# Marks for expert gates: comparisons one step ahead of the dots, Pool's low halves in quarters, sixteen dots moved

## The reference, cut to what matters

```
def peer_ffn(x, wq, subkeys, u, v):
    q = (xt @ wq).reshape(t_len, PEER_HEADS, 2, PEER_QDIM // 2)
    sub = einsum('thpd,hpkd->thpk', q, subkeys)          # 8 heads, 2 halves, 128 keys
    s_top, i_top = top_k(sub, 16)
    cand = s_top[:, :, 0, :, None] + s_top[:, :, 1, None, :]
    sc, ci = top_k(cand.reshape(t_len, 8, 256), 16)
    i1 = take_along_axis(i_top[:, :, 0], ci // 16); i2 = take_along_axis(i_top[:, :, 1], ci % 16)
    eid = i1 * 128 + i2                                  # 128 experts for each token
    gate = softmax(sc)
    h = gelu(einsum('cd,ced->ce', xc, u[eid]))
    return einsum('ce,ced->cd', gate * h, v[eid])
```

## Time and profile before

| what | us |
|---|---|
| median of three runs | 1715.17 |
| the profiled execution | 1707.7 |
| its span | 1705.9 |
| PE busy | 1651.9 (97%) |
| VectorE busy | 1251.1 (73%) |
| ScalarE busy | 691.9 (41%) |
| Pool busy | 831.9 (49%) |
| PE's mean granted clock | 0.988 of full speed |

### The profile page before, as it was taken

The page is one execution under the profiler, slowest core; times in us unless marked ns, Lnnn a source line. Parts: engine busy times, 40 slices in busy tenths (PEclk is TensorE's granted clock), DMA queues, the critical chain, the costliest instruction groups (busy, mean ns, idle before and its releaser), DMA issues.

```text
span 1705.9 us, 24150 instructions
## 1 busy us (share of the span) xinstructions
PE 1651.9 (97%) x9013; PEld 1449.1 (85%) x9013; DVE 1251.1 (73%) x2462; ACT 691.9 (41%) x1030; POOL 831.9 (49%) x492
## 2 busy tenths in 40 slices
PE   9999999999999998899989989999999999999997
PEld 7778777788899998899989988999888888888886
DVE  3586894421255795999999999535888888888886
ACT  4545545422324344343443434333433333333332
POOL 6332233344633676776876677785524223332312
PEclk9999999999999999999999999999999999999999
DMA  5121122242422566997899689997999999999952
GB/s 203 63 75 62 50 75 74 87 148 87 161 74 71 177 208 236 343 379 233 291 379 364 222 290 367 375 372 284 394 401 354 375 382 358 375 376 353 385 200 86
DMA packets 126499, 417.61 MB, mean 245 GB/s; under 512 B 12976, under 2 KB 32432, under 8 KB 124848
## 3 DMA queue, kind: packets, MB, share of 16 engines
q1 hardware_dynamic: 70320, 232.81, 38.2%
q0 software_dynamic: 36864, 134.23, 21.0%
q10 hardware_dynamic: 19200, 49.03, 7.5%
HBM read 364.91 MB, written 50.86 MB: 244 GB/s over the span
## 4 chain that ended last, share of the span: by engine, by line
PE 76%; DVE 12%; DMA 5%; POOL 3%; issue 2%; ACT 2%; ACTq 0%; SPq 0%; DVEq 0%; POOLq 0%
PE ps L1362 14%; PE ps L1364 13%; PE ps L1363 13%; PE ps L1622 10%; PE ps L1621 10%; PE ps L1624 10%; DMA u_got<-u_rows,eid 4%; DVE right L1256 3%; DVE u_got L1126 2%; POOL w_lo L503 1%; PE ps L1474 1%; PE ps L1426 1%; POOL w_lo L459 1%; DMA raw<-w_units 1%; PE ps L1733 1%
## 5 line engine op out<-in xcount | busy, mean ns | idle before, releaser
L1362 PE MATMUL ps<-tok_hi,w_hi 128*128 128x384 f32 (+1 forms) x1472 | 531.1, 361 | 1.5 <-issue 1.5
L1364 PE MATMUL ps<-tok_hi,w_lo 128*128 128x384 f32 (+1 forms) x1472 | 521.7, 354 | 0.0
L1363 PE MATMUL ps<-tok_lo,w_hi 128*128 128x384 f32 (+1 forms) x1472 | 521.6, 354 | 0.0
L560 ACT ACTIVATE w_hi<-raw 128x1024 fp32r<-128x1024 f32 x330 | 349.2, 1059 | 391.0 <-PE ps L1624 288.4
L503 POOL TENSOR_TENSOR w_lo<-raw,w_hi 128x1024 fp32r<-128x1024 f32 x128 | 322.7, 2523 | 113.7 <-ACT w_hi L560 112.4
L459 POOL TENSOR_TENSOR w_lo<-raw,w_hi 128x1024 fp32r<-128x1024 f32 x76 | 182.2, 2401 | 315.0 <-ACT w_hi L560 314.9
L1362 PEld LDWEIGHTS ps<-tok_hi,w_hi 128*128 128x128 f32 x1472 | 280.4, 190 | 32.0 <-issue 12.3
L520 POOL DMA_INDIRECT v_got<-v_rows,eid x128 | 153.9, 1203 | 300.1 <-DVE own L1138 281.7
L1621 PE MATMUL ps<-w_hi,gh_hi 128*128 128x512 f32 x760 | 295.7, 389 | 0.0
L1622 PE MATMUL ps<-w_lo,gh_hi 128*128 128x512 f32 x760 | 295.7, 389 | 0.0
L1364 PEld LDWEIGHTS ps<-tok_hi,w_lo 128*128 128x128 f32 x1472 | 279.8, 190 | 18.1
(11 more groups left out here) (247 smaller groups left out, 1806.2 us busy)
## 6 DMA issues: line engine op xcount, KB each, us to landing
raw<-u_units SPq DMA_DIRECT2D x128, 512.0 KB, 4.7
raw<-v_rows SPq DMA_DIRECT2D x128, 512.0 KB, 6.7
raw<-w_units SPq DMA_DIRECT2D x78, 512.0 KB, 3.4
gate_d<-stage ACTq DMA_DIRECT2D x12, 2048.0 KB, 10.6
gelu_d<-gelu_t ACTq DMA_DIRECT2D x120, 192.0 KB, 4.7
gelu_in<-gelu_d SPq DMA_DIRECT2D x30, 768.0 KB, 8.1
gate_in<-gate_d SPq DMA_DIRECT2D x28, 768.0 KB, 12.5
gate_in<-gate_d SPq DMA_DIRECT2D x2, 1536.0 KB, 17.0
```

The source lines that it names most:

```text
L560: act.activation(hi_of(n), raw[:, n % RAW, :], ACT.Copy).then_inc(hi_done, 1)
L1362: pe.matmul(out_, l_hi, r_hi, start=start, stop=False)
L1363: pe.matmul(out_, l_hi, r_lo, start=False, stop=False)
L1364: return pe.matmul(out_, l_lo, r_hi, start=False, stop=stop)
```

## The change

Three edits. Pool makes each low half of the expert units in four subtractions of 256 columns; only the last tells the others. VectorE's `mark` is cut in two: `mark(m)` makes the comparisons (`match`, `left`), `times_gates(m)` the two products; in a mark stage the comparisons of mark m + 1 stand right behind the products of mark m, ahead of the dots of that unit. A semaphore of its own tells TensorE that `left` is set. The dots of the mark stages go from 30 to 26 each, those of routing tiles 2 and 3 from six to four; what is left comes in the tail.

```
+LO_PARTS = 4
-ROUTE_DOTS, MARK_DOTS = (3, 6, 6), 30
+ROUTE_DOTS, MARK_DOTS = (3, 4, 4), 26
...
                 pool.wait_ge(hi_done, n + 1)
-                pool.tensor_tensor(w_lo[:, n % RAW, :], raw[:, n % RAW, :], w_hi[:, n % RAW, :].bitcast(F32),
-                                   ALU.subtract).then_inc(lo_pool, 1)
+                for a in range(LO_PARTS):
+                    cols = slice(a * DM // LO_PARTS, (a + 1) * DM // LO_PARTS)
+                    ins = pool.tensor_tensor(w_lo[:, n % RAW, cols], raw[:, n % RAW, cols],
+                                             w_hi[:, n % RAW, cols].bitcast(F32), ALU.subtract)
+                ins.then_inc(lo_pool, 1)
...
+            def spread(a, m):
+
+                first = MARKED * (m % (P // MARKED))
+                return marks[:, a, first:first + MARKED].rearrange("p (g t) -> p g t", t=2).unsqueeze(2)\
+                    .to_broadcast([P, MARKED // 2, P, 2])
+
             def mark(m):
 
                 if m == 0:
                     dve.wait_ge(numbers_set, 1)
                 if m >= 3:
                     dve.wait_ge(gate_full, 2 * (m - 2))
                 if m >= 2:
                     dve.wait_ge(right_set, m - 1)
-                dve.tensor_tensor(match[:, m % 2], each, second, ALU.is_equal).then_inc(match_set, 1)
-                dve.tensor_tensor(left[:, s], each, first, ALU.is_equal)
+                each = numbers[:].unsqueeze(1).to_broadcast([P, MARKED // 2, P, 2])
+                dve.tensor_tensor(match[:, m % 2], each, spread(1, m), ALU.is_equal).then_inc(match_set, 1)
+                dve.tensor_tensor(left[:, m % 3], each, spread(0, m), ALU.is_equal).then_inc(left_set, 1)
+
+            def times_gates(m):
+
                 dve.wait_ge(match_set, m + 1)
                 for i in range(PIECES):
-                    ins = dve.tensor_tensor(right[i][:, s], match[:, m % 2], gate[i], ALU.mult)
+                    ins = dve.tensor_tensor(right[i][:, m % 3], match[:, m % 2], spread(2 + i, m), ALU.mult)
                 ins.then_inc(right_set, 1)
...
                 spread_picks(b)
+                mark(P // MARKED * (b - 1))
                 for k in range(MARK_UNITS):
-                    mark(P // MARKED * (b - 1) + k)
+                    m = P // MARKED * (b - 1) + k
+                    times_gates(m)
+                    if k + 1 < MARK_UNITS:
+                        mark(m + 1)
                     dots_to(dots_by(routed_at(b) + ROUTE_UNITS + k))
...
             def gates_of(q):
 
                 s = q // 2 % 3
+                pe.wait_ge(left_set, q // 2 + 1)
                 pe.wait_ge(right_set, q // 2 + 1)
```

More of the change, by code:

```diff
@@ L307, in peer_block @@
         "route_step", "gexp_in", "gexp_done", "pick_set", "pickT_full", "pickT_set"))
-    match_set, right_set, gate_full, gate_read, marks_step, numbers_set = (sem(n) for n in (
-        "match_set", "right_set", "gate_full", "gate_read", "marks_step", "numbers_set"))
+    match_set, left_set, right_set, gate_full, gate_read, marks_step, numbers_set = (sem(n) for n in (
+        "match_set", "left_set", "right_set", "gate_full", "gate_read", "marks_step", "numbers_set"))
     stage_out = [sem(f"stage_out{i}") for i in range(2)]
@@ L1238, in spread_picks @@
                 dve.wait_ge(marks_step, 2 * b)
+            def spread(a, m):
+                first = MARKED * (m % (P // MARKED))
+                return marks[:, a, first:first + MARKED].rearrange("p (g t) -> p g t", t=2).unsqueeze(2)\
+                    .to_broadcast([P, MARKED // 2, P, 2])
             def mark(m):
-                s, tok = m % 3, slice(MARKED * (m % (P // MARKED)), MARKED * (m % (P // MARKED)) + MARKED)
                 if m == 0:
@@ L1246, in mark @@
                     dve.wait_ge(gate_full, 2 * (m - 2))
-                first, second, *gate = (marks[:, a, tok].rearrange("p (g t) -> p g t", t=2).unsqueeze(2)
-                                        .to_broadcast([P, MARKED // 2, P, 2]) for a in range(2 + PIECES))
-                each = numbers[:].unsqueeze(1).to_broadcast([P, MARKED // 2, P, 2])
                 if m >= 2:
                     dve.wait_ge(right_set, m - 1)
-                dve.tensor_tensor(match[:, m % 2], each, second, ALU.is_equal).then_inc(match_set, 1)
-                dve.tensor_tensor(left[:, s], each, first, ALU.is_equal)
+                each = numbers[:].unsqueeze(1).to_broadcast([P, MARKED // 2, P, 2])
+                dve.tensor_tensor(match[:, m % 2], each, spread(1, m), ALU.is_equal).then_inc(match_set, 1)
+                dve.tensor_tensor(left[:, m % 3], each, spread(0, m), ALU.is_equal).then_inc(left_set, 1)
+            def times_gates(m):
                 dve.wait_ge(match_set, m + 1)
                 for i in range(PIECES):
-                    ins = dve.tensor_tensor(right[i][:, s], match[:, m % 2], gate[i], ALU.mult)
+                    ins = dve.tensor_tensor(right[i][:, m % 3], match[:, m % 2], spread(2 + i, m), ALU.mult)
                 ins.then_inc(right_set, 1)
```

## The result

The changed kernel takes **1768.82 us** (median of four runs, 1763.97 to 1769.71) against 1712.01 for the kernel before in the same comparison: ratio **1.0321** (95% interval 1.027 to 1.0372). It is 3.2% slower; the forecast was 1696. The profiled span is 1767.6 us against 1705.9.

The account below looks back on a forecast made before the run. PE was held up in the mark stages by VectorE, stalled by Pool's subtraction, with DMA a second limit. Marks -30 and tail +11 gave -19: 1707.7 to 1689, plus 7.5 for the median, 1696 us; range 1672 to 1716.

Parts of the forecast that it names:

- part one: Pool's expert low half in four pieces: 2.95 us instead of 2.40, a waiting VectorE instruction losing at most 0.74 instead of 2.4.
- I take one piece, 0.74: VectorE's stall per mark from Pool's pieces, chosen as 0.74 us between bounds of 0 and 2.95.
- A waiting engine is served next: At the port VectorE and Pool share: Pool got in between two adjoining VectorE instructions, so whichever engine waits goes next.
- Part two, order: Mark stages: comparisons moved ahead of the dots bring `right` 1.28 us earlier; the new waits on `gate_full` and `left_set` cost nothing.
- Part three, dots in the marks: Mark stages with 26 dots instead of 30: VectorE 5.5 us a unit, 87 us a stage; 30 us won.
- The wait for picks at the head of stage 3: Third mark stage's head unit takes 11.87 us instead of 5.15, PE waiting for routing's picks; these 6.7 us would go.
- DMA as second limit: Mark stages: DMA share 0.91 to 0.95, busy time with fewer dots 90.4, 85.6, 91.8 us; gain between 23 and 36 us.
- full pace: Rival: DMA carries it and mark units reach PE's 5.15 us; -52 + 6 gives 1669 us; chance 0.15.
- Tail: Last expert units: 16 added dots load Pool (4.95 to 5.50 us a unit) and DMA; 11 us lost, bounds 4 and 20.
- Turn by turn: Rival: most mark operations wait for a piece each, VectorE needs 6.9 us a unit; 1764 us; chance 0.08.
- its deciding point of 1.2 us: Stall per mark from which the marks' gain, 8 us, no longer pays for the tail and the kernel is slower.
- Pieces do not help: Rival: Pool retakes the port at once and VectorE waits for all four pieces; 1706 us; chance 0.10.

Follow-up runs that it names:

- x_pieces: The kernel before with only Pool's low half cut into four subtractions of 256 columns; order and dots as before: ratio 1.0035.
- x_order: The kernel before with only the new order of comparisons and products; low half whole, dots as before: ratio 1.0181.
- x_after_oldorder: The changed kernel with the new order alone undone; four pieces and moved dots kept: ratio 0.9982 to the kernel before.
- x_memset: The changed kernel with each of Pool's low-half subtractions replaced by a write of zeros, so the low halves are left out: one run, 1669.58 us.
- x_leftwait: The changed kernel with Pool waiting for the next mark's comparisons before each low half in the mark stages: ratio 0.9848 to the kernel before.
- x_whole: The changed kernel with the low half in one instruction again; new order and moved dots kept: ratio 1.0223 to the kernel before.
- x_dots: The kernel before with only the dots moved (26 per mark stage, 39 in the tail): ratio 0.9918.
- x_whole_leftwait: The changed kernel with the low half undivided and Pool waiting for the next mark's comparisons before it: ratio 0.9764 to the kernel before.
- x_left_olddots: `x_whole_leftwait` with the dots back at their old places, 30 per mark stage: ratio 0.9808 to the kernel before, 1680.94 us.
- x_tail_short: `x_whole_leftwait` with row gathers from row 94 on taking only 256 of 1024 columns: one run, 1665.79 us.
- x_gaps: The changed kernel with Pool waiting on a semaphore between pieces, setting them 0.08 us apart: ratio 0.9999 to the kernel before.

## Why the prediction was wrong, step by step

**The step that failed** is the one number of part one that I chose between far bounds: "I take one piece, 0.74", of 0 to 2.95 us of stall per mark. The measured stall is 154.1 - 48 x 0.68 = 121.5 us on `match` and 71.3 - 96 x 0.64 = 9.9 on the products: 131 us, **2.7 us per mark**, near the upper bound, where before it was 1.08. Two of its reasons fell. "A waiting engine is served next" holds for 22 of the 30 comparisons that come while a piece runs in `x_pieces`, but not for a VectorE instruction that starts about 0.3 us before the first piece: that one loses to all four, as it loses to a whole low half in `x_order`. The trace of the kernel before had it too: nine of its 96 products start 0.3 us ahead of a low half and take 3.2 us, since they wait for all of it. The first of them, merged with its undisturbed partner, and the low half (VectorE, then Pool):

```profile
675.69 3.83 DVE L1256 TENSOR_TENSOR right<-match,marks 128x1024 f16<-128x1024 f16 x2
```

```profile
676.01 2.35 POOL L503 TENSOR_TENSOR w_lo<-raw,w_hi 128x1024 fp32r<-128x1024 f32 x1
```

And "the collisions seen are of Pool's start with the last operations before the dots" took the place of the collisions for fixed, while the same change moved it.

**Part two, order, "nothing".** This is where that came from. The four operations do stay together, and around the cycle (dots, products, comparisons, dots) only the pairs have changed places; I asked who waits for `right` and `gate_full`, and not where Pool's low half falls in the new cycle. Pool waits for the slot that a dot frees (110.4 us, 42 times), gathers, and makes the low half a fixed time after that dot; after two products that is on the comparison, in 40 of 48 marks. Shown: the order alone costs 1.8% (`x_order`), added last 3.4% (`x_after_oldorder`); the collision alone is the cause (`x_memset`, and `x_leftwait`, which keeps all of Pool's work); the place is what matters (`x_leftwait`). Argued only: why the old order does not lock in the same way. Its stalled operation is the product PE waits for, so a stall delays PE, ScalarE's `w_hi` and with it the low half, which pushes Pool out of step. The waits fit: with the new order Pool waits for a dot 42 to 46 times in the mark and routing stretches (`x_order` and `x_whole` 46), in the old order 30 times in the kernel before, and 10 to 15 in `x_dots`, `x_pieces` and `x_after_oldorder`; and it waits for `w_hi` 29 and 45 times in the kernel before and `x_dots`, against 16 in the changed one. But with pieces in the old order that second count is low too (18 and 21, against 17 and 21 in `x_order` and `x_whole`), so the way out of step is not proved.

**Part one, the price of pieces.** Four take 2.80 us, not 2.95; an extra instruction costs (2.80 - 2.40)/3 = 0.13 us, not 0.184. The Trainium skill, "GPSIMD Engine Reference", section Instruction dispatch, put it at tens of cycles, by which the low half would have stayed near 2.5 us; the trace, 2.80, lies between it and me. More important, pieces alone gave no gain (1.0035): the stall was 1.6 us a mark against 1.08, so taking turns cost VectorE more than waiting once.

**Part three, dots in the marks.** Right in kind: alone they give 0.9918, marks of 87.9 and 87.7 us in stages 2 and 3, the 87 that I gave for VectorE. That agreement is luck: the stall there was still 1.1 us a mark and not 0.74. The wait for picks at the head of stage 3 went, 11.9 to 4.5, as forecast (worth 7.4 us and not 6.7, which I had counted against a unit with gates), but in `x_pieces` it went without the moved dots. In the changed kernel the shorter dots could not pay for the stall: VectorE's cycle is 1.21 (products) + 3.57 (`match`, start to start) + 0.60 + 1.625 x 1.14 (dots) = 7.2 us, 16 of them 115, which is stages 2 and 3.

**DMA as second limit.** The floors were wrong, and unseen in the result since VectorE hid them. I read the share of 0.91 to 0.95 as "DMA stays nearly full", with floors of 85.6 to 91.8 us a stage. `x_whole_leftwait` has the same 26 dots and stages of 83.9 and twice 82.6 us, at shares of 1.00, 0.97 and 0.96 and 390, 376 and 373 GB/s. At a share of 0.95 the kernel before had moved 352 in stage 2: nearly the same share, and fewer bytes. With 26 dots DMA did not stop PE's pace, and the rival "full pace" was right that far. But the limit is near: with 30 dots (`x_left_olddots`) the stages take 86.6 to 88.3 us with VectorE waiting for rows.

**Tail.** 16.4 us lost, forecast 11, bounds 4 to 20. But the reason was half wrong: I costed Pool's queue (4.95 to 5.50 us a unit). With pieces or without, the tail is the same: 103.8 and 106.4, 106.9 and 105.1. My second reason, the DMA time of 16 more gathers (12 us more), has the right kind by `x_tail_short`; that 11.5 us came off there is no proof of the size, as more bytes than those of 16 rows were left out. The waits agree: 50.8 us for rows and 24.4 for units, 11.6 for Pool.

**The rivals.** *Turn by turn* had 0.08, and gave 1764 against 1768.8. Its direction was right, its size partly by luck, its mechanism only in part: VectorE's time per unit did come to about 7 us by a stall of over 2.2, but by one operation waiting for all four pieces, not by turns. Where the turns do happen (`x_gaps`, `x_after_oldorder`) the stall is 1.5 and 1.6 us a mark and the kernel is at 1.00, so its deciding point of 1.2 us was somewhat low. With bounds of 0 to 2.95 around it, 0.08 was far too low all the same: most of the interval lay beyond it. *Pieces do not help* (0.10) had the mechanism of the collision, VectorE waiting for all four; but it took the number of collisions as it was and gave 1706, as it did not see either that the new order would bring one into nearly every mark.

## What to carry to other kernels

When two engines exclude each other, ask not only how long they collide but where in its cycle each arrives, and what fixes that: an engine that waits on the other's progress arrives at the same place every time, and a reordering that leaves the sum of the work alone can put that place on an operation that loses. Splitting the long instruction was no cure here: an instruction that was there before the first piece waited for all of them. Better is to couple the two on purpose, with a wait that puts the long instruction beside work that does not contend (here dots that read PSUM), which turned 1.032 into 0.985, and 1.022 into 0.976 with the low half undivided.

## What the runs showed of the hardware

- Starting first in the profile does not win: `match` at 702.97 lost to a Pool instruction that began at 703.26 (40 of 48 marks), and in `x_order` at 704.90 to one of 705.21 (41 of 48). Why is open; no run shows whether an instruction's start in the profile is the moment at which it asks for the exclusive part. In both, VectorE's products before it had ended 0.22 us or a little more ahead of Pool's start, and Pool's subtraction followed directly on its last gather (0.02 us).
- Four Pool instructions issued without a gap kept a VectorE instruction that had started before them out for all four (2.80 us); 0.08 us between them was enough to let it in behind the first, worth 3.2% (`x_gaps`).
- Pool writing zeros did not disturb VectorE (683 to 685 ns), and Pool's subtraction did not disturb a VectorE operation with one of its two inputs in PSUM (dots of 1.21 us in every kernel). The Trainium skill, "SBUF — State Buffer", section Who interferes with whom, describes an exclusive lock held by the engine that came first. The traces agree on the exclusion; the order of service is not that of the starts in the profile.
- The three mark stages of `x_whole_leftwait` moved 390, 376 and 373 GB/s over 83 to 84 us each, in stages 2 and 3 with PE never starved. This is above the 358 GB/s that the Trainium skill, "SBUF — State Buffer", section A bandwidth-pool intuition that's wrong, gives between HBM and one core.
